# A fused decoder step on one core: the planned order of the engines recomputed with new times, and all rows of the V table weighed on TensorE

## What is computed

```python
q = (hc @ w_q).reshape(PEER_CHUNK, PEER_HEADS, 2, PEER_QDIM // 2)
sc = jnp.einsum('chpd,hpkd->chpk', q, sub_keys)
s1, i1 = lax.top_k(sc[:, :, 0], PEER_TOPK)
s2, i2 = lax.top_k(sc[:, :, 1], PEER_TOPK)
cand = s1[..., :, None] + s2[..., None, :]          # 256 sums per token and head
top_s, pos = lax.top_k(cand, PEER_TOPK)             # 16 of them; eid: their expert numbers
gate = jax.nn.softmax(top_s, axis=-1)
act = jax.nn.gelu(jnp.einsum('cd,chkd->chk', hc, u[eid]))
return jnp.einsum('chk,chkd->cd', gate * act, v[eid])
```

## Time and profile before

| what | value |
|---|---|
| median of 3 executions | 3883.09 us (3873.05 to 3890.93) |
| profiled execution | 3865.63 us |
| its span | 3863.8 us |
| busy: TensorE, VectorE, GpSimd, ScalarE | 2715.3, 2532.2, 2339.2, 631.4 us |
| moved | 1295.70 MB, 335 GB/s over the span |
| mean granted clock of TensorE | 0.839 |

### The profile page before, as it was taken

How to read it: one execution, slowest core, us unless ns; L and a number is a source line. 1 busy time by engine, 2 the same in 40 slices (tenths; PEclk the granted TensorE clock), 3 DMA queues, 4 the chain that set the end, 5 groups by cost and what they waited for, 6 DMA issues and landing times.

```text
span 3863.8 us, 30640 instructions
## 1 busy us (share of the span) xinstructions
PE 2715.3 (70%) x7286; PEld 1323.9 (34%) x7286; DVE 2532.2 (66%) x6330; ACT 631.4 (16%) x1880; POOL 2339.2 (61%) x2076
## 2 busy tenths in 40 slices
PE   5866669687778777777798785457766566665665
PEld 3533335343434344334344343122332222222221
DVE  1467777677766677767667876555787555555553
ACT  2112212122211121212111121001111011110110
POOL 0155644476465577776745775444667777777774
PEclk7877879788899888888999888678987988888887
DMA  9799889899789899998988998777999999999997
GB/s 365 269 365 335 311 334 345 328 349 347 259 311 357 342 344 357 344 351 316 352 332 300 361 358 311 275 259 259 363 353 354 368 374 367 376 360 377 365 372 251
DMA packets 344554, 1295.70 MB, mean 335 GB/s; under 512 B 41880, under 2 KB 44784, under 8 KB 330912
## 3 DMA queue, kind: packets, MB, share of 16 engines
q0 software_dynamic: 298368, 1086.46, 76.2%
q1 hardware_dynamic: 46008, 207.29, 14.2%
HBM read 1272.76 MB, written 55.43 MB: 344 GB/s over the span
## 4 chain that ended last, share of the span: by engine, by line
POOL 24%; PE 24%; DMA 23%; issue 12%; DVE 9%; DVEq 3%; another core or an unknown queue 2%; ACT 1%; SPq 1%; ACTq 0%; POOLq 0%
DMA v_ring<-in_peer_v,idx 13%; POOL v_ring L1355 12%; POOL u_ring L1350 12%; PE acc L1594 12%; PE pS L1400 4%; DMA u_ring<-in_peer_u,idx 4%; PE pA L1526 3%; DMA wbuf<-zS_scr 2%; DVE u_ring L2204 2%; PE pS L1503 1%; DVE accs L2244 1%; DMA xbuf<-in_x_all 1%; PE pS L1442 1%; DMA o_all<-in_cache_swa 1%
## 5 line engine op out<-in xcount | busy, mean ns | idle before, releaser
L1594 PE MATMUL acc<-v_ring,diag 128*128 128x512 f32 x2820 | 1662.0, 733 | 861.0 <-DMA v_ring<-in_peer_v,idx 728.1
L1355 POOL DMA_INDIRECT v_ring<-in_peer_v,idx x1024 | 1191.3, 1163 | 772.3 <-PE acc L1594 355.4
L2204 DVE CUSTOM_DVE_ANT_0 u_ring<-u_ring,hb 128x1024 f32<-128x1024 f32 x1024 | 1244.7, 1222 | 577.8 <-DMA u_ring<-in_peer_u,idx 554.8
L1350 POOL DMA_INDIRECT u_ring<-in_peer_u,idx x1024 | 1123.5, 1097 | 713.3 <-issue 292.5
L1594 PEld LDWEIGHTS acc<-v_ring,diag 128*128 128x128 f32 x2820 | 605.5, 230 | 1748.6 <-issue 1603.1
L2244 DVE SCALAR_TENSOR_TENSOR accs<-v_ring,wv,accs 128x1024 f32<-128x1024 f32 x319 | 409.8, 1285 | 89.1 <-DMA v_ring<-in_peer_v,idx 57.4
L1832 ACT ACTIVATE diag<-idn,wv 128x128 f32<-128x128 f32 x705 | 264.8, 396 | 1160.1 <-PE acc L1594 818.9
L1400 PE MATMUL pS<-wbuf,T 128*128 128x512 f32 (+1 forms) x640 | 263.5, 562 | 22.7 <-DVE T L1927 16.0
L1526 PE MATMUL pA<-T,wbuf 128*128 128x256 f32 (+2 forms) x1280 | 256.4, 357 | 21.3 <-issue 15.6
L1526 PEld LDWEIGHTS pA<-T,wbuf 128*128 128x128 f32 x1280 | 221.2, 204 | 72.8 <-issue 46.6
L1400 PEld LDWEIGHTS pS<-wbuf,T 128*128 128x128 f32 x640 | 123.0, 197 | 142.7 <-issue 129.5
(11 more groups left out here) (224 smaller groups left out, 1908.4 us busy)
## 6 DMA issues: line engine op xcount, KB each, us to landing
wbuf<-in_w_in SPq DMA_DIRECT2D x40, 1024.0 KB
wbuf<-in_w_q SPq DMA_DIRECT2D x40, 1024.0 KB
out_dil_s<-in_cache_dil SPq DMA_DIRECT2D x8, 4092.0 KB
wbuf<-in_w_out SPq DMA_DIRECT2D x20, 1024.0 KB
u_ring<-in_peer_u,idx POOLq DMA_INDIRECT x1024
v_ring<-in_peer_v,idx POOLq DMA_INDIRECT x1024
xbuf<-in_x_all SPq DMA_DIRECT2D x16, 512.0 KB
wbuf<-in_w_in SPq DMA_DIRECT2D x10, 512.0 KB
```

Source lines behind the costliest of these rows:

```text
L1350: pool.indirect_dma_start(u_ring[:, entry % RU, :], None, table, bass.IndirectOffsetOnAxis(rows, 0))\
L1355: pool.indirect_dma_start(v_ring[:, entry % RV, :], None, peer_v, bass.IndirectOffsetOnAxis(rows, 0))\
L1594: m = pe.matmul(acc[0:R, half * 512:(half + 1) * 512], w, v_ring[:, entry % RV, half * 512:(half + 1) * 512], start=first, stop=last, skip ...
L2204: dve.tensor_tensor_reduce(row, row, hb[:, t % 2, :], 1.0, 0.0, ALU.mult, ALU.add, dots[:, section % 2, j:j + 1]).then_inc(u_used, 1)
```

## The change

1. `times_of` and `pick_line` get shorter times for TensorE: a z stage 2.0 us instead of 3.6, an output projection 4.0 instead of 7.2, a query stage 1.2 or 2.1 instead of 3.4 or 4.0, transposes of a tile 1.6 instead of 3.3, a weighing 1.25 instead of 1.98, and so on.
2. All V rows are weighed on TensorE (`self.on_pe[p] = True`), and `load`, which made the choice, is gone.
3. The sample rows' `smul` and `spv` are not planned before FETCH = 12 us after the last use of the buffer.
4. `deadlines` sets marks for every head of a tile, not only for the first, and a ranking of a tile is not planned before the `idx` slot that it takes over is free (five slots).

The hardware program keeps all its kinds of steps; it loses line 2244 and what goes with it.

```diff
@@ times_of @@
-        return (("PE", 1.9 if a[0] == "kva" else 3.6),)
+        return (("PE", 1.1 if a[0] == "kva" else 2.0),)
...
-        return (("PE", 7.2),)
+        return (("PE", 4.0),)
...
-        "ht": (("PE", 3.3),), "hv": (("ACT", 1.3),),
-        "q": (("PE", 3.4 if len(group) == 1 else 4.0),), "qe": (("ACT", 0.36),), "k": (("PE", 0.45 * len(group)),),
+        "ht": (("PE", 1.6),), "hv": (("ACT", 1.3),),
+        "q": (("PE", 1.2 if width_of(group) < 2 * P else 2.1),), "qe": (("ACT", 0.36),), "k": (("PE", 0.2 * len(group) + 0.1),),
@@ deadlines @@
-            n = self.given[t, 0]
-            if n > marks[-1][0]:
-                marks.append((n, max(p - 10, 1)))
+            for h in range(HEADS if t != SAMPLE else 1):
+                n = self.given[t, h]
+                if n > marks[-1][0]:
+                    marks.append((n, max(p + TOPK * h - 10, 1)))
@@ pick_line @@
-                out += [("weigh", p, 1.98)] if pick_v(p) is not None else []
+                out += [("weigh", p, 1.25)] if pick_v(p) is not None else []
@@ ready_stage @@
+        if BASE[n][0] in ("smul", "spv") and BASE[n][2] == 0:
+
+            m = n - 1 if BASE[n][0] == "spv" or BASE[n][1] == 0 else AT["smul", BASE[n][1] - 1, 1]
+            if BASE[n][0] == "spv" and BASE[n][1] == 0:
+                m = AT["smul", NS - 1, 1]
+            if BASE[n][0] == "spv" and BASE[n][1] > 0:
+                m = AT["spv", BASE[n][1] - 1, 0]
+            end = self.part_end.get((m, 0))
+            if end is None:
+                return None
+            ready = max(ready, end + FETCH)
+        if BASE[n][0] == "r3":
+
+            for t in BASE[n][6]:
+                if OI[t] >= SLOTS and ("fsum", ORDER[OI[t] - SLOTS]) not in self.ends:
+                    return None
@@ send @@
-            at = self.landed[g]
-            pe, dve = max(self.free["PE"], at - 6.0) + self.load("PE", p), max(self.free["DVE"], at - 6.0) + self.load("DVE", p)
-            self.on_pe[p] = pick_v(p)[0] == "s" or pe + 0.6 <= dve
+            self.on_pe[p] = True
```

More of the change, by code:

```diff
@@ L41 @@
 SC_SLOTS = 4
+SLOTS = 5
+SLOT = {t: i % SLOTS for t, i in OI.items()}
 PLACE_IN_GROUP = {t: s for g in GROUPS for s, t in enumerate(g)}
@@ L68, in rows_of, with width_of @@
     return NS if t == SAMPLE else P
+def width_of(group):
+    return sum(rows_of(t) for t in group)
 def prompt_of(group):
@@ L260, in times_of @@
     return {
[L261 removed]
+        "xg": (("DVE", 2.7),), "zt": (("PE", 0.3 if a == "kva" else 0.8),),
         "zv": (("ACT", 0.35 if a == "kva" else 0.65),),
[L263 to L265 removed]
+        "s": (("PE", 0.6 if first else 0.6 + 0.13 * n),), "sm": (("DVE", 1.9 if first else 1.3 + 0.14 * n),),
@@ L266, in times_of @@
+        "se": (("ACT", 1.4 if first else 1.3 + 0.12 * n),), "p": (("PE", 0.6 if first else 0.5 + 0.18 * n),),
+        "pe": (("ACT", 0.5 if first else 0.9 + 0.12 * n),), "v": (("PE", 0.5 if first else 0.5 + 0.14 * n),),
         "vd": (("DVE", 0.6),), "vo": (("ACT", 0.6),),
-        "n1": (("ACT", 1.5),), "n2": (("DVE", 2.9),), "n3": (("ACT", 1.3),), "nt": (("PE", 3.3),), "ng": (("ACT", 2.4),),
+        "n1": (("ACT", 1.5),), "n2": (("DVE", 2.9),), "n3": (("ACT", 1.3),), "nt": (("PE", 1.6),), "ng": (("ACT", 2.4),),
@@ L395 @@
 PACE = 2.9
+FETCH = 12.0
 class Planner:
@@ L578, in ready_pick @@
         return None
-    def load(self, e, p):
-        out = 0.0
-        for kind, q, time in self.picks[e][self.pick[e]:self.pick[e] + 40]:
-            place = q if kind in ("dot", "weigh", "diag") else None
-            if place is not None and place >= p:
-                break
-            if kind == "weigh" and self.on_pe.get(q) != (e == "PE"):
-                continue
-            out += time
-        for n, i, time in self.parts[e][self.base[e]:self.base[e] + 12]:
-            if self.by[n] <= p:
-                out += time
-        return out
     def send(self):
@@ L714 @@
 STAGED = {x: i for i, x in enumerate(x for x in Z_ITEMS if x[0] in ("qa", "qb") and 0 < x[1] < NT)}
-SLOTS = 5
-SLOT = {t: i % SLOTS for t, i in OI.items()}
 R3 = [s for s in BASE if s[0] == "r3"]
 RANKED = {(t, s[2]): i + 1 for i, s in enumerate(R3) for t in s[6]}
-def width_of(group):
-    return sum(rows_of(t) for t in group)
 X_LOADS = (("sq", 0), ("sq", 1), ("sq", 2), ("o", 0), ("sq", 3), ("sq", 4), ("o", 1), ("o", 2), ("sq", 5), ("sq", 6),
```

10 lines of the change are left out of this document (3 added, 7 removed).

## The result

| what | before | after |
|---|---|---|
| median of 4 executions, measured side by side | 3878.14 us | 3986.89 us (3983.82 to 3992.57) |
| ratio, 95% interval | | 1.0277 (1.0247 to 1.0307) |
| span of the profiled execution | 3863.8 us | 3982.0 us |
| moved | 1295.70 MB | 1295.86 MB |
| mean granted clock of TensorE | 0.839 | 0.932 |

The change made the kernel 2.8% slower; 1.1% was forecast.

What follows compares the result with a forecast made beforehand. DMA engines bound it, most in the tail (2.86 us per place). First stretch +96, sample rows -60, end +8 make +44 on the 3863.8 us span; with 1.8 around it and 17.5 to the median, 3927 us, range 3790 to 4040.

Steps and rivals of the forecast that it cites:

- part 1: First stretch, from first gather to 29th idx write: 207 places move to the tail, TensorE becomes longest; +96 us.
- I take 0.90: TensorE's assumed busy share in the first stretch: 1475 us of work takes 1639 us.
- The even price: First stretch must shrink from 2135 to 1543 us, since 207 places move to the tail at 2.86 us each.
- Sample rows: Stretch where sample rows run: FETCH lets dot products fill idle DMA time; -60 us, between 0 and -84.
- cost 0: Tail: TensorE takes all weighings, 586 of 700 us, without slowing the places.
- part 3: All V rows on TensorE: tail cost 0, +8 us at the end, most of its cost held in part 1's 1475 us.
- The offset to the median: Median of the kernel before lay 17.5 us above its profiled execution; added to 3910 to give 3927 us.
- TensorE has room: Rival: overlapping matmul records overstate TensorE's work in the first stretch; faster, 3800 us, chance 0.27.
- The queues lock: Rival: late weighings free V slots late and queues wait on each other; first stretch 1799 us, total 4087, chance 0.15.
- The tail turns over: Rival: TensorE's clock stays at half in the tail, 3.75 us per place; about 4325 us, chance 0.03.
- Nothing moves: Rival: sample-row gains and the loss ahead of them cancel; 3883 us, chance 0.10.
- rival 2: The queues lock; its sign was TensorE below 85% in the first stretch with waits for V rows or maxima; chance 0.15.

Runs made afterwards that it cites:

- e2: The change with the old TensorE planner times, all V rows still on TensorE: 3796.63 us, ratio 0.9797 to the kernel before.
- e5: The kernel before with the FETCH rule alone added: 3796.18 us, ratio 0.9774.
- r1: The change, unedited, run again on the first chip: 3975.84 us, ratio 1.027 to the kernel before.
- e1: The change with the choice of weighing engine restored (789 of 1032 V rows on TensorE): 3925.86 us, ratio 1.0119 to the kernel before.
- e3: The change with old times and choice of weighing engine restored, leaving FETCH, marks and slot rule: 3758.71 us, ratio 0.9696 to the kernel before.
- e10: The change with traced TensorE times and the choice of weighing engine restored: 3785.94 us, ratio 0.9801 to the kernel before.
- r6: The change, unedited, run on the third chip: 3879.69 us, ratio 1.0138 to the kernel before.

## Why the prediction came out as it did

**The direction and its reason held.** The sum was made of a first stretch that gives up 207 places and doesn't shrink by their price, sample rows that gain, and a tail at the old price. All three are in the traces, with those signs, and undoing the times alone removes the loss (e2: -4.8 points). The size did not hold: +44 us on the span against +118.

**The step that failed is in part 1: the share that TensorE reaches, "I take 0.90".** The work was right: 1475 us forecast, 1458 measured to 1862 us, with the weighing at 1.95 as taken and the clock at 0.93. But 1458 us of work took 1697, a share of 0.86, where 0.90 gave 1639: +58, of the 74 us that the sum lacked. I set one mean share from two rows, 91.6% and 86%, and took the stretch as one regime. It is three. Under projections TensorE is 92 to 95% busy and the gathers starve, since up to five stages stand between weighings and there are four V slots. Under the first heads behind them TensorE is 72 to 81% busy, stands for fetched queries and for the chain of a head, and the weighings stand behind. Elsewhere the gathers run nearly as before: between 700 and 1050 the DMA share is 0.89. I had the order with those blocks in front of me (10 weighings where 22 stood) and priced it through TensorE's total, which doesn't change with the sequence. What the sequence cost is 142 us of DMA time in 570 us. The lower of my two figures, 86%, came out, but as a mean over these three regimes, and so by chance.

**The even price** was right: the 574th dot product is done at 2300 us, and the stretch would have had to shrink to 1543.

**Sample rows**: -60 forecast, -51 measured, and the tail with the end +16 where +8 was forecast. The waits of VectorE for keys fell from 70.6 us to this, in the stretch 1855 to 2481:

```profile
DVE wbuf L2123 <- DMA wbuf<-zS_scr: 18.3, 7, 5.6
DVE wbuf L2123 <- DMA xbuf<-zS_scr: 13.8, 1, 13.8
```

e5 shows that FETCH alone gained 75 there in the order with the old times. I had capped it at the stretch's 84 us of idle DMA time and deducted 24 for what may stay idle; with FETCH alone less stayed idle than that, in the change more.

**V rows on TensorE**: the tail's "cost 0" nearly held, 2.90 against 2.86 us per place; the tail and the end together cost 16 us, and 1 in r1. That "part 3 costs most in part 1's sum" is what e1 shows: 1.6 points there, 1.0 with the old times and nothing measurable with the traced ones.

**The offset to the median** was luck: 17.5 us were added for it, and the median of after lies 3 us above its profiled execution. So the 74 us that the sum lacked (118 - 44) became 60 in the time (3986.9 - 3927).

**Rivals.** *TensorE has room* fell: its share stopped at 86%. The Trainium skill (Perfetto Trace Analysis, section Identifying the Most-Contended Engine) judges TensorE's headroom by weight-load busy time, and by the share of peak FLOP/s, which was not worked out here. Weight loads are 51.23 of 110 us, 47%, in the stretch 1590 to 1700, where matmul records fill 98% and the timeline from 1640 to 1662 has no gap between them. As a sign of room for more work the trace doesn't agree with it. *The queues lock* had more of the mechanism than I gave it, at 60% of its price: GpSimd stood 550.9 us for V slots, longest 31.1, and the first stretch came to 1697 us, not 1799. In the projections it was no chain, stages simply stood ahead of weighings; behind them, weighings stood behind steps that TensorE waited for (25.21 us at 1179.97). *The tail turns over* fell: the clock is 0.98 from 3300 to 3700 us. Moving VectorE's rows is what raised it: in the same stretch it is 0.96 in e2 and 0.82 in e3, which differ in that alone. *Nothing moves* fell.

**The signs** named beforehand: clock above 0.90 (0.93), DMA share near 0.82 (0.81), last `idx` write near 2420 us (2481), 2.86 us per place after (2.90), no key wait over a few us (5.6, but for one of 13.8). TensorE "near 90%" missed (85.8%), just above the 85% that was named for rival 2.

**Open**: what is left of Q, since the kernels don't nest; why the first heads have so few weighings beside them; the gain of marks and slot rule; and the cost of all V rows on TensorE from the kernel before alone was not run. Why old times, which overstate transposes and queries, do a little better than traced ones where the choice stands (e3 against e10, in two sets) isn't settled either.

## What to carry to other kernels

A planner's times are not a forecast but a rule for what goes ahead of what. Too short a time for an engine that is shared by long steps and by steps that free buffers lets the long ones pack together, and the engine that fills the buffers stands still while the shared one looks busy. Look at the stretch behind the pack too: here half of the loss was there. Price such a change by stretch: its time, less its places at the price of a place where nothing else runs. Take the time of a step from its own record; counts in short stretches, added up, count a record twice that lies across a border. Undo the parts one by one before you judge them, since here one part's gain of 2.1 points hid nearly half of another's loss.

## Unexpected of the hardware

Chips differ in how fast they gather, and orders feel it differently. In the stretch 3300 to 3700, the change's order moved this on the first chip (r1) and on the third (r6):

```profile
3300.00:3700.00 400.00, 281.26 (x564) 99.50 (x563) 185.75 (x336) 55.52 (x149) 301.18 (x282) 0.97 0.98 372
```

```profile
3300.00:3700.00 400.00, 295.80 (x594) 106.20 (x592) 196.73 (x356) 59.47 (x160) 302.97 (x298) 0.97 1.01 391
```

The profiles of the first chip lie between 362 and 374 GB/s there. From r1 to r6 the span lost 93 us, 81 of them in the tail, which went from 1487 to 1406 us. The tail of the kernel before is 920 us; at the same rate it would gain 50 (an estimate, as it was not profiled on the third chip), and its time fell by 42. So the kernel that has put more of its places into the tail profits more: the same pair of kernels gave 1.027 on one chip and 1.0138 on the other, intervals apart. A ratio to the same kernel before does not take the chip out.
